# A gather for the first 128 tokens of an expert layer, beside a dense product for the other 384

## The reference

```
q = (h2 @ peer_wq)                       # 8 heads, two halves of 128 each
v1, i1 = top_k(q_left  @ peer_k1, 16)    # of 128 keys, for each token and head
v2, i2 = top_k(q_right @ peer_k2, 16)
sc, ci = top_k(v1[:, None] + v2[None], 16)
experts = i1[ci // 16] * 128 + i2[ci % 16]     # 8 x 16 = 128 experts for each token, of 16384
gates = softmax(sc)
z   = einsum('td,tkd->tk', h2, peer_u[experts])
act = gelu(z) * gates
y2  = einsum('tk,tkd->td', act, peer_v[experts])
x   = layer_norm(ALPHA * x + gate2 * y2, ln2_g, ln2_b)
```

## Time and profile before

| | |
|---|---|
| median of the runs | 3963.03 us |
| the profiled execution's span | 3955.0 us |
| busy: TensorE / weight loads / VectorE / ScalarE / GpSimd | 3616 / 2972 / 2115 / 1500 / 1535 us |
| moved by DMA | 445 MB, 113 GB/s in the mean |

### The profile page before, as it was taken

The page is one execution under the profiler, slowest core; times in us unless marked ns, Lnnn a source line. Parts: engine busy times, 40 slices in busy tenths (PEclk is TensorE's granted clock), DMA queues, the critical chain, the costliest instruction groups (busy, mean ns, idle before and its releaser), DMA issues.

```text
span 3955.0 us, 49618 instructions
## 1 busy us (share of the span) xinstructions
PE 3616.2 (91%) x19382; PEld 2971.9 (75%) x19382; DVE 2114.9 (53%) x3633; ACT 1500.4 (38%) x2360; POOL 1535.4 (39%) x724
## 2 busy tenths in 40 slices
PE   6988789999998889989885899989999999999998
PEld 6876668887766778866673588768978888888886
DVE  4375656565446475245768629998852333323335
ACT  4545443324334333225332423337643222322232
POOL 6633224443223234433210243433444545445452
PEclk9999899999999999999885899999999999999999
DMA  6411124443212134322100124445564444444442
GB/s 196 158 57 64 43 71 153 144 134 107 72 57 86 54 116 133 103 93 64 38 2 22 53 78 128 128 125 195 208 213 145 158 137 159 147 141 161 139 149 74
DMA packets 298039, 445.37 MB, mean 113 GB/s; under 512 B 8144, under 2 KB 219088, under 8 KB 295760
## 3 DMA queue, kind: packets, MB, share of 16 engines
q1 hardware_dynamic: 278640, 371.22, 28.6%
q0 software_dynamic: 19168, 70.98, 5.5%
HBM read 383.45 MB, written 58.72 MB: 112 GB/s over the span
## 4 chain that ended last, share of the span: by engine, by line
PE 74%; DVE 16%; issue 4%; ACT 3%; POOL 2%; DMA 1%; POOLq 0%; DVEq 0%; SPq 0%; ACTq 0%
PE bank L441 21%; PE bank L443 21%; PE bank L442 21%; PE bank L2710 3%; PE bank L522 2%; DVE arena_rw L2238 2%; POOL split_low L427 2%; DVE arena L2798 1%; PE bank L1744 1%; DVE arena L2800 1%; DVE arena L2804 1%; PE bank L1768 1%; DVE arena L2891 1%; PE bank L2042 1%; DVE arena L2802 1%
## 5 line engine op out<-in xcount | busy, mean ns | idle before, releaser
L427 POOL TENSOR_TENSOR split_low<-weights,split_high 128x1024 fp32r<-128x1024 f32 x554 | 1391.7, 2519 | 2160.0 <-ACT split_high L419 2153.8
L441 PE MATMUL bank<-normed_high,split_high 128*128 128x512 f32 x2352 | 940.1, 400 | 70.7 <-issue 38.8
L442 PE MATMUL bank<-normed_low,split_high 128*128 128x512 f32 x2352 | 926.1, 394 | 0.0
L443 PE MATMUL bank<-normed_high,split_low 128*128 128x512 f32 x2352 | 925.0, 393 | 0.0
L419 ACT CAST split_high<-weights 128x1024 fp32r<-128x1024 f32 x554 | 574.6, 1047 | 630.3 <-PE bank L443 536.4
L441 PE MATMUL bank<-hidden_high,split_high 128*128 128x512 f32 x1536 | 600.4, 391 | 6.4 <-ACT hidden_high L2793 4.2
L443 PE MATMUL bank<-hidden_high,split_low 128*128 128x512 f32 x1536 | 598.7, 390 | 0.0
L442 PE MATMUL bank<-hidden_low,split_high 128*128 128x512 f32 x1536 | 598.5, 390 | 0.0
L441 PEld LDWEIGHTS bank<-normed_high,split_high 128*128 128x128 f32 x2352 | 449.0, 191 | 175.7 <-issue 65.1
L443 PEld LDWEIGHTS bank<-normed_high,split_low 128*128 128x128 f32 x2352 | 448.1, 191 | 95.6
L442 PEld LDWEIGHTS bank<-normed_low,split_high 128*128 128x128 f32 x2352 | 449.0, 191 | 93.6 <-issue 2.6
(11 more groups left out here) (411 smaller groups left out, 4832.8 us busy)
## 6 DMA issues: line engine op xcount, KB each, us to landing
weights<-in_w_ff SPq DMA_DIRECT2D x64, 1024.0 KB, 5.5
weights<-in_peer_u SPq DMA_DIRECT2D x64, 1024.0 KB, 5.9
weights<-in_peer_v SPq DMA_DIRECT2D x64, 1024.0 KB, 5.1
gate_table<-arena SPq DMA_DIRECT2D x16, 2048.0 KB, 7.4
gates<-gate_table POOLq DMA_DIRECT2D x32, 1024.0 KB, 9.8
weights<-in_cond_w SPq DMA_DIRECT2D x24, 1024.0 KB, 5.5
early_table<-branch SPq DMA_DIRECT2D x72, 256.0 KB, 2.1
lates<-early_table POOLq DMA_DIRECT2D x18, 1024.0 KB, 11.2
```

What stands on the lines that cost most here:

```text
L427: pool.do.tensor_tensor(lo, raw_unit(u), hi.bitcast(F32), ALU.subtract).then_inc(*pool.sig("split_low", u))
L441: pe.do.matmul(o, ah, bh, start=first, stop=False)
L442: pe.do.matmul(o, ah, bl, start=False, stop=False)
L443: return pe.do.matmul(o, al, bh, start=False, stop=last)
```

## The change

Tokens 0 to 127 leave the dense path. After their search the numbers of their 128 experts are kept (`own_expert`). GpSimd gathers, for each of the 128 choices k, one row of peer_u for each token by an indirect DMA (128 rows of 4 KB, token on the partition), and VectorE multiplies it with the token's h2 (turned by TensorE into the two banks `twin`) and sums, one `tensor_tensor_reduce` for each k. 32 of these stand in each of the later search rounds, 32 in the gate stage. After Gelu and gate, the rows of peer_v are gathered likewise and VectorE adds `row * act` into `twin`, five for each group of the down products. TensorE turns the sum back once at the end.

The other 384 tokens stay dense: matmuls, Gelu, tables, gating and sums have 384 columns, the gate stage has 48 batches. All 128 up tiles now precede the down products, and all go through the early table: 18, 27, 27, 27 in the search rounds, 23 among the batches, 6 after them. The engines no longer meet. The loads of a group's hidden values and gates are issued from ScalarE's queue, one group ahead. Two of the eight banks (`twin`) are held throughout.

```diff
-EARLY_GROUPS = 18
 HOT = 8
-SEARCH_TILES = 12
+WIDE = T - P
+EXPERT_TILES = EXPERT_GROUPS * GROUP
+ROUND_TILES = (18, 27, 27, 27)
+TAIL_TILES = 6
+ROUND_DOTS = 32
+U_RING, V_RING = 4, 7
...
-        bank_tiles = [ctx.enter_context(nc.psum_tensor(f"bank{i}", [P, 512], F32))[:, :] for i in range(8)]
+        twin = ctx.enter_context(nc.psum_tensor("twin", [P, 1024], F32))[:, :]
+        bank_tiles = [twin[:, 0:512], twin[:, 512:1024]]
+        bank_tiles += [ctx.enter_context(nc.psum_tensor(f"bank{i}", [P, 512], F32))[:, :] for i in range(2, 8)]
...
+        for g in range(EXPERT_GROUPS):
             W["P", "up", g] = up(dram["peer_u"], g)
-        n_late = EXPERT_GROUPS - EARLY_GROUPS
-        order = sorted(range(EXPERT_GROUPS), key=lambda g: ((g + 1) / EARLY_GROUPS if g < EARLY_GROUPS
-                                                            else (g - EARLY_GROUPS) / n_late))
...
+        for g in range(EXPERT_GROUPS):
+            W["P", "down", g] = down(dram["peer_v"], g)
...
-        early = Ring([y[:, c, :] for c in range(CT)], marks)
...
+        early = Ring([y_buf[:, j * WIDE:(j + 1) * WIDE] for j in range(5)], marks)
...
+        near = [place(f"rows_near{j}", 17344 + j * D, D) for j in range(2)]
+        u_rows = [place(f"rows_y{j}", 12288 + 2048 + j * D, D) for j in range(2)] + near
+        v_rows = [place(f"rows_arena{j}", A + 12288 + j * D, D) for j in range(5)] + near
...
+        HOTS = range(P // HOT, T // HOT)
+        LAST_GATE = 2 * HOTS[-1] + 1
+        MIDDLE_TILES = EXPERT_TILES - sum(ROUND_TILES) - TAIL_TILES
+        MIDDLE_DOTS = HK - (TT - 1) * ROUND_DOTS
...
+            for g in range(EXPERT_GROUPS):
+                yield from pe_product(("early", g), W["P", "up", g], wide_tile, h_ready(PM), lambda c: [("gelu", g, c)],
+                                      WIDE)
...
+        def u_due(t):
+            start = ROUND_TILES[0]
+            searched = sum(ROUND_TILES)
+            if t < start + 1:
+                return 0
+            if t < searched:
+                return U_RING + (TT - 1) * ROUND_DOTS * (t - start) // (searched - start)
+            return U_RING + (TT - 1) * ROUND_DOTS + MIDDLE_DOTS * (t - searched) // MIDDLE_TILES
+        def rows_at(n):
+            return 0 if n == 0 else max(0, min(5, HK - 5 * (n - 1)))
+        def rows_before(n):
+            return sum(rows_at(i) for i in range(n))
...
+            for j in range(2):
+                bank, empty = banks.take_at(j, "own_rows", j)
+                pe.wait_ge(empty)
+                for i in range(4):
+                    o, c = bank[:, i * P:(i + 1) * P], 4 * j + i
+                    pe.do.matmul(o, h_hi[:, c, 0:P].bitcast(F32), identity, start=True, stop=False)
+                    last = pe.do.matmul(o, h_lo[:, c, 0:P].bitcast(F32), identity, start=False, stop=True)
+                last.then_inc(*pe.sig("own_rows", j))
...
+            for n in range(EXPERT_GROUPS):
+                hi, lo = wide_hidden[n % 2]
+                run(pe_product((PM, "down", n), W["P", "down", n], lambda k: (hi[:, k, :], lo[:, k, :]),
+                               lambda a: [at("hidden_high", PM, n, a), at("hidden_low", PM, n, a)],
+                               lambda c: [("y_sum", PM, n, c)], WIDE))
+                if n == ROWS_END:
+                    for j in range(2):
+                        bank, empty = banks.take("own_turned", j)
+                        pe.wait_ge(empty, at("own_kept", j))
+                        for i in range(4):
+                            last = pe.do.transpose(bank[:, i * P:(i + 1) * P], v_rows[0][:, (4 * j + i) * P:(4 * j + i + 1) * P],
+                                                   identity)
+                        last.then_inc(*pe.sig("own_turned", j))
+                        banks.give(("own_turned", j), ("own_sum", j))
...
+            for n in range(EXPERT_GROUPS):
+                for c in range(GROUP):
+                    act.wait_ge(at("gated_hidden", n, c), at("product", (PM, "down", n - 2), CT - 1) if n > 1 else None)
+                    act.do.copy(wide_hidden[n % 2][0][:, c, :], lates[n % 2][:, c, :]
+                                ).then_inc(*act.sig("hidden_high", PM, n, c))
+                    if c == 0 and n < EXPERT_GROUPS - 1:
+                        act_expert_loads(n + 1)
+                if n:
+                    act_down(W["P", "down", n - 1], end)
...
+        def act_expert_loads(n):
+            act.wait_ge([early_written(n, c) for c in range(GROUP)],
+                        at("hidden_low", PM, n - 2, GROUP - 1) if n > 1 else at("gate", LAST_GATE))
+            act.do.dma_start(lates[n % 2], early_table[n * GROUP:(n + 1) * GROUP].rearrange("c p t -> p c t")
+                             ).then_inc(*act.land(f"lates_landed{n % 2}", n))
             act.wait_ge(table_written(N_BLOCKS - 2), table_written(N_BLOCKS - 1))
...
+            act.do.dma_start(gates[n % 2].rearrange("p b a t -> p b (a t)"), gate_table.rearrange("b p n -> p b n")
+                             [:, :, n * GROUP * STAGE_TOKENS:(n + 1) * GROUP * STAGE_TOKENS]
+                             ).then_inc(*act.land(f"gates_landed{n % 2}", n))
...
+        def dve_dots():
+            dve.wait_ge(at("own_rows", 0), at("own_rows", 1))
+            for k in range(HK):
+                rows = u_rows[k % U_RING]
+                dve.wait_ge(at(f"u_landed{k % U_RING}", k))
+                dve.do.tensor_tensor_reduce(out=rows, in0=rows, in1=twin, scale=1.0, scalar=0.0, op0=ALU.mult, op1=ALU.add,
+                                            accum_out=own_z[:, k:k + 1]).then_inc(*dve.sig("own_dot", k))
+                yield
...
+        def dve_rows():
+            for k in range(HK):
+                rows, act_k = v_rows[k % V_RING], own_z[:, k:k + 1]
+                dve.wait_ge(at(f"v_landed{k % V_RING}", k), at("own_act") if k == 0 else at("own_row", k - 1))
+                if k == 0:
+                    dve.do.tensor_scalar(twin, rows, act_k, None, ALU.mult).then_inc(*dve.sig("own_row", k))
+                else:
+                    dve.do.scalar_tensor_tensor(out=twin, in0=rows, scalar=act_k, in1=twin, op0=ALU.mult, op1=ALU.add
+                                                ).then_inc(*dve.sig("own_row", k))
+                yield
...
+                fill(dots, shared_out(MIDDLE_DOTS, m))
+            run(dots)
+            dve.wait_ge(at("own_gelu"))
+            dve.do.tensor_tensor(own_z, own_z, own_gate, ALU.mult).then_inc(*dve.sig("own_act"))
+            rows = dve_rows()
+            for n in range(EXPERT_GROUPS):
+                hi, lo = wide_hidden[n % 2]
                 for c in range(GROUP + 1):
                     if c < GROUP:
...
+                        s = lates[n % 2][:, c, :].rearrange("p (b t) -> p b t", t=STAGE_TOKENS)
+                        dve.wait_ge(at(f"lates_landed{n % 2}", n), at(f"gates_landed{n % 2}", n))
+                        dve.do.tensor_tensor(s, s, gates[n % 2][:, :, c, :], ALU.mult
+                                             ).then_inc(*dve.sig("gated_hidden", n, c))
                     if c:
...
                         dve.wait_ge(at("hidden_high", PM, n, c - 1))
...
+                        dve.do.tensor_tensor(lo[:, c - 1, :], lates[n % 2][:, c - 1, :], hi[:, c - 1, :].bitcast(F32),
+                                             ALU.subtract).then_inc(*dve.sig("hidden_low", PM, n, c - 1))
                 if n:
...
+                    dve_wide_down(n - 1, rows, rows_at(n))
...
+        def dve_wide_down(n, rows, n_rows):
+            for c in range(CT):
+                made, total = banks.tile("product", (PM, "down", n), c)[:, 0:WIDE], y[:, c, P:]
+                dve.wait_ge(at("product", (PM, "down", n), c))
+                if n:
+                    dve.wait_ge(at("y_sum", PM, n - 1, c))
+                    dve.do.tensor_tensor(total, total, made, ALU.add).then_inc(*dve.sig("y_sum", PM, n, c))
+                else:
+                    dve.wait_ge([early_written(k // GROUP, k % GROUP) for k in range(EXPERT_TILES - 5, EXPERT_TILES)])
+                    dve.do.tensor_copy(total, made).then_inc(*dve.sig("y_sum", PM, n, c))
+                if c < n_rows:
+                    next(rows)
+                if n == EXPERT_GROUPS - 1:
+                    dve_block_sum("block1", 1, c, at("y_sum", PM, n, c), at("own_sum", c // 4), at("block_out", "block0", c))
...
+        def dve_own_experts():
+            dve.wait_ge(at("work_free", 0))
+            dve.do.scalar_tensor_tensor(out=half_f[:, 0:HK], in0=parts3[:, 0:HK], scalar=float(NKEYS),
+                                        in1=parts3[:, HK:2 * HK], op0=ALU.mult, op1=ALU.add).then_inc(*dve.sig("dve_step"))
+            dve.wait_ge(dve.last)
+            dve.do.tensor_copy(own_expert, half_f[:, 0:HK]).then_inc(*dve.sig("own_expert"))
...
+        def pool_u_rows():
+            for k in range(HK):
```

(84 more changed lines are left out.)

171 lines of the change are left out of this document (68 added, 103 removed).

## The result

The change makes the kernel slower: 4008.76 us (median of 4 runs, 4006.84 to 4009.99) against 3963.36 for the kernel before on the same chip, a ratio of 1.0117 with an interval of 1.0104 to 1.0129: 1.2% slower, clear of the noise. The profiled span is 4006.9 us, against 3955.0. Forecast were a span of 3701 and a time of 3705. So 306 us of span are missing from the working.

The account below looks back on a forecast made before the run. Before the change TensorE bounds gate and experts stages, VectorE the search. Search ends at 2803, gate stage 3005, passage 3033, experts 3624, end 3674; plus 15 and 12, span 3701; with 8 more 3709, stated 3705 us, range 3615 to 3850.

Parts of the forecast that it names:

- The matmul's width: Up and down products on TensorE: 384-column matmuls start 173.3 ns apart, 328 us less over 6144 matmuls.
- C: Rival on TensorE: weight loads bind at 191 ns a matmul, 3745 us; chance 0.05.
- Durations on VectorE: Dots and row sums over 1024 columns: 1225 ns for a dot plus 83 ns for reading its sum, row sums alike.
- The gather on GpSimd: Each indirect DMA costs GpSimd 1.2 us, between ends of 0.54 and 2.40, and stays hidden, but barely.
- B: Rival: a gather costs GpSimd 2.0 to 2.4 us; 3777 us at 2.2, 3822 at 2.4; chance 0.22.
- D: Rival: slower than before, a gather's issue on GpSimd taking 3 us or more; 4088 us at 3.5; chance 0.07.
- Search: Search rounds: VectorE sets each of three later rounds at 119.1 us, 357 us together.
- the allowance: Search rounds: 12 us added because splits come 1.4 times as often and stop VectorE's two-operand instructions; 123 us a round.
- Gate stage: Gate tables: VectorE takes 202 us, from 48 batches of 3.30 and 32 dots of 1.36; TensorE 182.
- DMA: Experts: DMA engines bound the 26 groups with rows at 18.9 us each, 491 us; the other six take 16.6.
- What is queued behind the waits: Work waiting behind gathers: four in flight at one per 3.7 us bear a 14 us landing; cost priced at nothing.
- Rival E: Gathers don't overlap, a row comes each 5 us; round 160 us, group 25, total 3963 us; chance 0.04.

Follow-up runs that it names:

- f_gate_lead: On c_v_lead, the rows of u in the gate stage are sent three gathers earlier: 3755.11 us, ratio 0.9477 to the kernel before.
- e_dots_only: On c_v_lead, the 128 gathers of u are left out and the 128 dots stay, on cleared buffers: 3710.77 us.
- b_gather_only: Changed kernel with all 256 gathers, each waiting for the landing of the one a ring before it; no dots or row sums: 3633.27 us.
- c_v_lead: Changed kernel with the rows of v sent three gathers earlier, nothing else: 3815.43 us, ratio 0.963 to the kernel before.

## Why the prediction was wrong

By its own steps:

- **The matmul's width**: right to the digit (173.3 ns). Groups without rows 16.6: right. C falls with it.
- **Durations on VectorE**: right (1.208 + 0.083 and 1.287). **The gather on GpSimd**: 0.955, within its ends and below the 1.2 taken. The reason given for 1.2, addresses fetched one by one, no run shows; measured is 0.42 us more than for a plain DMA with as many rows. B and D are wrong as mechanisms, although D had the sign.
- **Search**: 119.1 forecast, 123 with the allowance; 128.6 measured. Of the 9.5 over the bare sum 4.9 come back with a lead of two. Without gathers the round is 116.7. In total this is 3 x 5.6 = 17 us of the miss.
- **Gate stage**: 202 forecast, 297 measured, 95 us of the miss. f_gate_lead gives back 75. Of the other 20, 14 are VectorE's own amount, sized too small (216 with no gathers of u at all), and 6 are left of the gathers. The sum took the tables of a batch over from the kernel before (1.22 + 1.22 + 0.93 = 3.37 us of instructions); in e_dots_only they take 4.11 on the mean, and the second table stands for up to 3.4 us beside one of GpSimd's splits, of which 23 now meet 48 batches where 24 met 64.
- **DMA**: a group with rows was priced at 18.9 us from a mix of rates (350 and 323 GB/s); b_gather_only shows 364, 17.3 us. The sentence of the Trainium skill on 358 GB/s (SBUF — State Buffer, "A bandwidth-pool intuition that's wrong") gave 17.6, an estimate, and was nearer than my rows; the trace agrees with it within 2%. What I had from busy shares of half-filled stretches was no measure of a full one. But this erred the other way, and hid part of the miss: 26.6 us a group lie 9.3 over the bytes and 7.7 over the forecast. That c_v_lead's groups come to 19.0, next to the forecast 18.9, is luck: the bytes take 17.3, and VectorE's waits are in it.
- **What is queued behind the waits**: this is the step that failed, and it carries some 190 us in the experts (the down products run from 3180.0 to 3975.5, 795.5 us for a forecast of 591 + 15) and most of the 95 in the gate stage. With the 17 of the search these are 302 of the 306. The prediction says "Four gathers in flight at one per 3.7 us bear a landing of 14 us", and prices the waits behind the gathers at nothing. The landing was even shorter than allowed (6.2 us). What was wrong is "in flight", for the seven buffers of v above all: I read the depth of the ring as the lead, and did not put GpSimd's sending point and VectorE's using point on one count. `due` is in the diff: that row 5n goes out at the first step of group n, where VectorE needs it at once, needs no chip. The same step looked at a waiting GpSimd, the consumer's release of a buffer, and not at a waiting VectorE, behind which ScalarE's casts, the splits and the next gathers stand.

Rival E had the right kind of cause, landings that set the pace, with 25 us a group against 26.6; but its mechanism is refuted: gathers overlap, and b_gather_only moves the same bytes at full rate.

One cost stands behind the waits. After such a pause TensorE's clock was at its lower level. Windows of the kernel after, first behind a pause of 5.7 us:

```profile
3495.00:3500.00 5.00, 5.00 (x16) 5.00 (x17) 3.21 (x4) 0.00 (x0) 4.29 (x3) 0.50 0.78 272
3501.00:3506.00 5.00, 5.00 (x31) 5.00 (x30) 4.23 (x6) 0.00 (x0) 0.00 (x0) 1.00 0.32 102
```

The granted clock is 0.50 (1.2 GHz), and 16 matmuls start in 5 us where 31 do at 1.00. This is some 2.5 us of lost work for this pause. Its share in the 190 us was not taken apart; with a lead of three the clock is 1.00 (the window of c_v_lead).

## What to carry to other kernels

Of a prefetch in an engine's ordered program, count the lead and not the depth of the ring: write the number of the last item sent and the number of the item needed as functions of the same loop counter, and put the difference, in time, against a landing. Do it for the first item of a turn too, and not only for the last. Then ask what stands behind the consumer if it has to wait, and whether that leads back to the issuer. If it does, the lateness is paid in each turn of the ring, and here no engine looked busy.

## What the runs showed of the hardware

- 134 MB of 4 KB rows gathered beside all other loads cost 36 us of span; the DMA engines held 364 GB/s over 300 us at a share of 1.04.
- A gather of 128 rows costs GpSimd 0.955 us, in the rounds and in the experts alike, but 1.27 to 1.35 on the mean in the gate stage, where VectorE reads two operands from SBUF, and 1.48 to 1.52 there in f_gate_lead. The rule of the Trainium skill (SBUF — State Buffer, "SBUF: two separate sides"), by which I had priced a hold of 2.25 us a gather, agrees in direction; the size is 0.3 to 0.6 us, and no run shows that VectorE is what holds the gather.
- A gather in the experts stage landed 6.2 us (median; 4.2 to 9.9) after its issue at a DMA share of 0.71, and 7.3 (4.5 to 10.5) in b_gather_only, at 1.04 in its full stretch.
